# Hybrid decoder trunk, two layers on one core: weight remainders and weight-block sums on VectorE, own semaphores for late cells, the sigmoid first in the gated output, layer 1's right sums in its projection

## The reference

```python
for i in range(2):
    h = rmsnorm(x, norm_mix[i])
    x = x + (even_mixer if i % 2 == 0 else odd_mixer)(h, ...)
    h = rmsnorm(x, norm_ffn[i])
    g = causal_dwconv(h @ w_gate[i], conv_w[i], conv_b[i])        # width 3, d_ff = 2816
    x = x + (gelu(g) * (h @ w_up[i])) @ w_down[i]
    gate = sigmoid(rmsnorm(x, norm_ple[i]) @ w_ple_gate[i])
    x = x + gate * (p[i] @ w_ple_proj[i])
```

## Time and profile before

| | before |
|---|---|
| median of 3 executions | 3092.41 us (3090.21 to 3092.66) |
| the profiled execution | 3093.49 us, its span 3091.7 us |
| mean granted TensorE clock | 0.993 |
| PE busy | 97% |
| DVE, ACT, POOL busy | 72%, 47%, 41% |
| DMA, mean | 113 GB/s |

### The profile page before, as it was taken

One profiled execution on the slowest core, in us unless ns is written; L12 is line 12 of the kernel. 1 busy time (PEld: TensorE's weight loads), 2 busy tenths in 40 slices (PEclk: granted clock), 3 DMA queues, 4 the chain that ended last, 5 costly groups with the idle time before them and its releaser, 6 DMA issues. The chain is left out here.

```text
span 3091.7 us, 44204 instructions
## 1 busy us (share of the span) xinstructions
PE 2989.6 (97%) x14830; PEld 2497.6 (81%) x14830; DVE 2238.8 (72%) x3533; ACT 1441.8 (47%) x3127; POOL 1269.5 (41%) x837
## 2 busy tenths in 40 slices
PE   7999999999999999999999999999999999999999
PEld 6778888978878878878888888899887887878877
DVE  5599997889377888789843331899548877879852
ACT  4385436878253333344432211888534333334431
POOL 3105545465235555511122545677325555630020
PEclk9999999999999999999999999999999999999999
DMA  5323334222314563375211334333122465266411
GB/s 176 127 58 101 99 123 108 50 56 68 130 66 145 156 139 108 133 262 194 84 55 41 105 97 140 82 68 75 48 90 91 157 157 138 82 227 225 154 55 48
DMA packets 288087, 349.07 MB, mean 113 GB/s; under 512 B 88316, under 2 KB 181292, under 8 KB 287916
## 3 DMA queue, kind: packets, MB, share of 16 engines
q1 hardware_dynamic: 274860, 312.27, 32.1%
q0 software_dynamic: 13056, 34.60, 5.2%
HBM read 268.70 MB, written 112.20 MB: 123 GB/s over the span
## 5 line engine op out<-in xcount | busy, mean ns | idle before, releaser
L2171 DVE TENSOR_SCALAR_CACHE_REDUCE k_x<-k_x,l0in_cand,l0in_want 128x384 bf16<-128x384 f32 (+1 forms) x186 | 174.9, 1003 | 1.2 <-DVE l0in_before L2166 0.2
L78 PE MATMUL l1in_acc<-k_w_lo,k_hi 128*128 128x512 f32 x384 | 150.9, 393 | 2.4 <-PEq L99 2.4
L80 PE MATMUL l1in_acc<-k_w_hi,k_hi 128*128 128x512 f32 x384 | 150.1, 391 | 0.0
L79 PE MATMUL l1in_acc<-k_w_hi,k_lo 128*128 128x512 f32 x384 | 150.0, 391 | 0.0
L2662 POOL TENSOR_TENSOR l0ff_w_lo<-l0ff_raw_g,l0ff_w_hi 128x512 fp32r<-128x512 f32 x64 | 90.7, 1424 | 133.2 <-ACT l0ff_w_hi L2520 132.6
L2662 POOL TENSOR_TENSOR l1ff_w_lo<-l1ff_raw_g,l1ff_w_hi 128x512 fp32r<-128x512 f32 x64 | 90.8, 1426 | 132.8 <-ACT l1ff_w_hi L2520 132.1
L2549 ACT ACTIVATE k_x<-k_x 128x512 f32<-128x512 f32 x88 | 55.6, 632 | 187.9 <-DVE k_x L2754 175.7
L721 DVE TENSOR_TENSOR l1in_sq<-l1in_out 128x512 f32<-128x512 f32 x32 | 38.4, 1201 | 107.9 <-ACT l1in_out L658 107.9
L1632 DVE TENSOR_TENSOR l1dil_pt_lo<-l1dil_ring,l1dil_pt_hi 128x512 fp32r<-128x512 f32 x192 | 102.0, 553 | 4.7 <-ACT l1dil_pt_hi L1568 2.3
L1648 DVE CUSTOM_DVE_ANT_0 l1dil_s<-l1dil_s,l1mix_sliding 128x128 f32<-128x128 f32 (+7 forms) x128 | 97.3, 761 | 8.5 <-PE l1dil_s L1732 5.6
L2710 DVE TENSOR_TENSOR l0ff_w_lo<-l0ff_raw_u,l0ff_w_hi 128x512 fp32r<-128x512 f32 x65 | 62.3, 958 | 56.6 <-ACT l0ff_w_hi L2520 56.6
(11 more groups left out here) (739 smaller groups left out, 11093.4 us busy)
## 6 DMA issues: line engine op xcount, KB each, us to landing
...
k_raw<-in_w_in_odd SPq DMA_DIRECT2D x24, 512.0 KB, 4.0
l0ff_raw_g<-in_w_gate SPq DMA_DIRECT2D x11, 1024.0 KB, 5.5
l0ff_raw_u<-in_w_up SPq DMA_DIRECT2D x11, 1024.0 KB, 6.5
...
l1ff_raw_g<-in_w_gate SPq DMA_DIRECT2D x11, 1024.0 KB, 5.5
```

Source lines behind the costliest of these rows:

```text
L78: pe.matmul(out, a_hi, b_lo, start=start, stop=False)
L79: pe.matmul(out, a_lo, b_hi, start=False, stop=False)
L80: return pe.matmul(out, a_hi, b_hi, start=False, stop=stop)
L2171: tick(dve.tensor_scalar(hits[:, cols], score[:, cols], cand[:, i:i + 1].bitcast(F32), want[:, i:i + 1], ALU.is_ge, ALU.add, accum_out=exc ...
```

## The change

1. In `ffn_stage` all lows go to VectorE, but for step 4 of group 0 and those of the down projection; so do all weight sums of groups 1 to 10. POOL keeps the sums of group 0.
2. The right sums stay in the feed-forward stage in layer 0 alone (`here`). Layer 1's are issued in its projection stage, copies behind the lows of strips 1 and 2, adds behind those of strips 3 and 4, chunks 0 to 2 of each.
3. The cells that are loaded late get semaphores of their own (`a11_late`, `a12_late`), which are waited for at cells 6, 7 and 8.
4. In the gated output ACT does unit 0's sigmoid before the squares, two squares go between the first two splits, the other two to unit 1, the later splits one unit later; TensorE runs the gate matmuls of unit 1 before unit 0's projection; VectorE's product waits for the projection itself.

```diff
@@ projection_stage, POOL
                     low(CH * s + c)
+                    if s in (1, 2) and c < 3:
+                        right_sums.copy(pool, 3 * s - 3 + c)
+                    if s in (3, 4) and c < 3:
+                        right_sums.add(pool, 3 * s - 9 + c)
@@ ple_stage, ACT
             p_round(1)
-            for t in range(ROOTS, NT):
-                feed.square(act, t)
+            act.wait_ge(begun, 1)
+            act.activation(sg[:, 0, :], ps_g[:, 0, :], ACT.Sigmoid).then_inc(sig_done, 1)
             split(0)
+            for t in range(ROOTS, ROOTS + 2):
+                feed.square(act, t, junk[:])
             split(1)
             for i, (s, t) in enumerate(UNITS):
                 if i in TURN_AFTER:
                     feed.round(act, TURN_AFTER[i])
...
-                if i < CH - 2:
-                    split(2 + i)
+                if i == 1:
+                    for t2 in range(ROOTS + 2, NT):
+                        feed.square(act, t2, junk[:])
+                if 0 < i <= CH - 2:
+                    split(1 + i)
@@ ple_stage, VectorE
                 dve.wait_ge(sig_done, i + 1)
+                dve.wait_ge(filled, i + 1)
@@ ple_stage, TensorE
             p_turn(0)
             p_turn(1)
+            gate(1)
             for i, (s, t) in enumerate(UNITS):
                 if i >= 2:
                     pe.wait_ge(prod_done, i - 1)
...
+                    gate(i)
@@ ffn_stage, SP
-                    load_part(a11, (0, 0), range(7, 8), a11_in)
-                    load_part(a12, (0, 1), range(6, 8), a12_in[0])
+                    load_part(a12, (0, 1), range(6, 8), a12_late)
+                    load_part(a11, (0, 0), range(7, 8), a11_late)
@@ ffn_stage, POOL
-                if q + L < Q and (q + L) % 2 == 0:
-                    low(q + L)
-                if n in (11, 12) and grp + 1 < NG:
-                    add_weights(grp + 1, 7, n - 11)
-                if n in (11, 13) and grp + 1 < NG:
-                    add_weights(grp + 1, 5, (n - 11) // 2)
-                if grp and n in (0, 1):
-                    add_weights(grp, 6, n)
-                if n in (3, 4):
+                if grp == 0 and n in (3, 4):
                     add_weights(grp, 3, n - 3)
-                if n in (2, 12) and 1 <= grp <= 6:
+                if here and n in (2, 12) and 1 <= grp <= 6:
                     i = 2 * ((grp - 1) % 3) + (n == 12)
                     right_sums.copy(pool, i) if grp <= 3 else right_sums.add(pool, i)
@@ ffn_stage, VectorE
                 if r == 0 and k == 0:
-                    dve.wait_ge(a11_in, 16 * 8)
+                    dve.wait_ge(a11_in, 16 * 7)
...
-                if q + L < Q and (q + L) % 2 == 1:
+                if q + L < Q:
                     low(q + L)
+                if n in (11, 12) and grp + 1 < NG:
+                    add_weights(grp + 1, 7, n - 11)
+                if n in (11, 13) and grp + 1 < NG:
+                    add_weights(grp + 1, 5, (n - 11) // 2)
+                if 0 < grp < NG and n in (0, 1):
+                    add_weights(grp, 6, n)
+                if 0 < grp < NG and n in (3, 4):
+                    add_weights(grp, 3, n - 3)
```

More of the change, by code:

```diff
@@ L152, in square @@
             act.wait_ge(self.squared, n)
-        act.activation(self.norm.junk, self.src[:, t, :], ACT.Square, accum_out=self.norm.ss[:, t:t + 1]).then_inc(self.squared, 1)
+        act.activation(junk if junk is not None else self.norm.junk, self.src[:, t, :], ACT.Square, accum_out=self.norm.ss[:, t:t + 1]).then_inc(self.squared, 1)
     def prepare(self, pool):
@@ L1205, in p_turn, with gate @@
                 mm.then_inc(p_turned, 1)
+            def gate(i):
+                s, t = UNITS[i]
+                tok = buf.slot(t)
+                for k in range(KD):
+                    if s == 1 and t == 0 and k % 2 == 0:
+                        pe.wait_ge(lo_ready, k // 2 + 1)
+                    mm3(pe, ps_g[:, i % 2, :], hi[:, tok, k, :], lo[:, tok, k, :], buf.x_hi[s][:, k, :], buf.x_lo[s][:, k, :], k == 0, k == KD - 1)
             p_turn(0)
             p_turn(1)
+            gate(1)
             for i, (s, t) in enumerate(UNITS):
@@ L1211, in _ @@
                     pe.wait_ge(prod_done, i - 1)
-                if t >= AHEAD:
-                    feed.ready(pe, t)
-                tok = buf.slot(t)
-                for k in range(KD if i else 0):
-                    if s == 1 and t == 0 and k % 2 == 0:
-                        pe.wait_ge(lo_ready, k // 2 + 1)
-                    mm3(pe, ps_g[:, i % 2, :], hi[:, tok, k, :], lo[:, tok, k, :], buf.x_hi[s][:, k, :], buf.x_lo[s][:, k, :], k == 0, k == KD - 1)
+                    if t >= AHEAD:
+                        feed.ready(pe, t)
+                    gate(i)
                 if s == 1 and t == 0:
@@ L2442, in _ @@
                     sp.wait_ge(filled, Q - 2)
-                    load_part(a11, (0, 0), range(8, 11), a11_in)
+                    load_part(a11, (0, 0), range(8, 11), a11_late)
                     load_part(a12, (0, 1), range(8, 9), a12_in[1])
@@ L2709, in low, with add_weights @@
                 dve.wait_ge(w_hi_done, q - buf.BEGUN + 1)
-                dve.tensor_tensor(buf.ring_lo[q % R][:], operand(q), buf.ring_hi[q % R][:].bitcast(F32), ALU.subtract).then_inc(w_lo_done[1], 1)
+                if q == 6:
+                    dve.wait_ge(w_lo_done[0], 3)
+                dve.tensor_tensor(buf.ring_lo[q % R][:], operand(q), buf.ring_hi[q % R][:].bitcast(F32), ALU.subtract).then_inc(w_lo_done[q % 2], 1)
+            def add_weights(grp, f, m):
+                n = 8 * grp + SUM_AT[f, m]
+                if f == 7:
+                    dve.wait_ge(raw_in[m], 16 * grp)
+                    dve.wait_ge(w_lo_done[m], 7 * grp + 1)
+                    dve.tensor_tensor(buf.piece(m, 0, 0), buf.piece(m, 0, 0), buf.piece(m, 1, 0), ALU.subtract).then_inc(w_sum, 1)
+                elif f == 5:
+                    dve.wait_ge(w_sum, n - 1)
+                    dve.tensor_tensor(buf.piece(m, 1, 0), buf.piece(m, 1, 0), buf.piece(m, 1, 1), ALU.add).then_inc(w_sum, 1)
+                elif f == 6:
+                    dve.wait_ge(w_sum, 8 * grp + SUM_AT[7, m])
+                    if grp == 0:
+                        dve.wait_ge(kept_stored[0], 16 * 6)
+                    dve.tensor_tensor(tmp[m], buf.piece(m, 1, 1), buf.piece(m, 0, 0), ALU.subtract).then_inc(w_sum, 1)
+                else:
+                    dve.wait_ge(w_sum, 8 * grp + SUM_AT[6, m])
+                    dve.wait_ge(w_lo_done[m], 7 * grp + 2)
+                    dve.tensor_tensor(buf.piece(m, 0, 1), buf.piece(m, 0, 1), tmp[m], ALU.subtract).then_inc(w_sum, 1)
             def corner(grp, m):
@@ L2779, in sum_left @@
                 if r == 0 and k == 0:
-                    dve.wait_ge(a11_in, 16 * 8)
+                    dve.wait_ge(a11_in, 16 * 7)
                 if r == 0 and k in (0, 8, 9):
                     n = max(k - 7, 0)
-                    dve.wait_ge(a12_in[n], 16 * (8, 1, 2)[n])
+                    dve.wait_ge(a12_in[n], 16 * (6, 1, 2)[n])
+                if r == 0 and k == 6:
+                    dve.wait_ge(a12_late, 16 * 2)
+                if r == 0 and k == 7:
+                    dve.wait_ge(a11_late, 16)
                 if r == 0 and k == 8:
-                    dve.wait_ge(a11_in, 16 * KB2)
+                    dve.wait_ge(a11_late, 16 * 4)
                 if r == 2 and k == 0:
@@ L3065, in trunk @@
                     Stage.used.extend(kept_stored + [filled])
-                    ffn_stage(nc, L + "ff", x, buf, ple, right_sums[layer], a["conv_w"][layer], a["conv_b"][layer], ident, acts, kept_stored, filled, begun)
+                    ffn_stage(nc, L + "ff", x, buf, ple, right_sums[layer], a["conv_w"][layer], a["conv_b"][layer], ident, acts, kept_stored, filled, begun, even)
                 recycle(nc)
```

18 lines of the change are left out of this document (11 added, 7 removed).

## The result

| | before | changed |
|---|---|---|
| median | 3091.49 us (4 runs, 3090.21 to 3092.66) | 3116.68 us (4 runs, 3114.69 to 3118.21) |
| ratio | | 1.0081, 95% interval 1.0069 to 1.0093 |
| profiled execution | 3093.49 us, span 3091.7 | 3118.21 us, span 3115.7 |
| mean granted clock | 0.993 | 0.987 |

The account below looks back on a forecast made before the run. TensorE was taken as the bound, busy 2989.6 of 3091.7 us. Terms -6.3 - 5.2 + 18.8 + 4 - 4.5 - 5.8 + 8 + 6 = +15.0 on the profiled 3093.5, stated as 3107 us, range 3075 to 3130.

Parts of the forecast that it names:

- the weight work on VectorE: Feed-forward: moving lows and weight sums from POOL removes the middle stretches' pauses, -6.3 us in layer 0, -5.2 in layer 1.
- the burst in layer 0: Feed-forward: unpaced, six right-sum copies then six adds go out together and delay raw-block loads, +18.8 us and +4 for clock.
- the gated output: Both layers: POOL's lows wait for all roots, so p loads late and gate(3) waits; +6 +2 and +4 +2 us.
- VectorE fits: Feed-forward: VectorE's 48 rows per group take 33.1 of 38.0 us, so it does not become the bound.
- the undisturbed row: 0.69 us per VectorE row without POOL's reads; the rival keeping the means had 47.5 us a group, 3280, milder 3127, chance 0.12.
- +18.8 + 4: Layer 0 feed-forward: late raw blocks of groups 1 and 2 cost 18.8 us, two falls of the clock 4.
- Group 1's first block lands near 932: Layer 0 feed-forward: that raw block lands near 932 instead of 925 beside the copies, holding VectorE's low and an eviction, +4.9 us.
- the 6.7: Layer 0 feed-forward: group 2's second block follows on the same queue another 11 us later, costing +6.7 us.
- In-order blocking: Feed-forward: VectorE waits in order at a group's first low for the raw block, with evictions of TensorE's banks queued behind.
- on POOL, where nothing else was urgent: Feed-forward: where each group's first low stood before the change, so its wait for the raw block held up nothing urgent.
- Layer 1's right sums: Layer 1 projection: issued behind the lows while POOL stands idle 88 us, they cost 0, between -1 and +2 us.
- The late cells: Start of the down projection: own semaphores end sum_left(0)'s wait for two unread cells, -4.5 us in layer 0, -5.8 in layer 1.

Follow-up runs that it names:

- the paced runs: Runs holding right-sum DMAs until TensorE has filled their steps; the first, the changed kernel with layer 0's twelve paced, measured 3092.93 us, ratio to before 1.0008.

## Why the prediction was right, and where its sizes were off

**The direction and the mechanisms.** Forecast 3107 in a range of 3075 to 3130, measured 3116.7. All three mechanisms that the sum rested on are in the trace and hold when each is undone or made alone: the weight work on VectorE is a gain (-16.1 alone), the burst in layer 0 a loss larger than it (23.8 come back when it is paced, and it costs 15.4 with its copies alone), the gated output a loss in both layers (+16.6 alone).

**VectorE fits.** 48 rows of 0.69 us were to give 33.1 of 38.0 us, 87%; the window 1011 to 1320 has 83%. The choice between the mean of before and the undisturbed row was the right one: with POOL idle the lows have a mean of 0.69. By the rule of the Trainium skill cited in the forecast ("SBUF — State Buffer", Who interferes with whom) this was to be expected, and the trace agrees: 0.69 with POOL idle, and in before 1.11 beside POOL against 0.68.

**The burst was mis-sized**, +18.8 + 4 against 15.8 + 9.2 = 25.0 of pauses and some 4 of half clock, and that the sum came so near is in part luck: the first pause was put at 4.9 and was 15.8, what follows the second burst was put at 5.9 + 6.7 + 1.3 = 13.9 and was 9.2.

The step that failed is "Group 1's first block lands near 932". It was split at 938.7. Three things are in the difference between the pauses. First, the forecast didn't use its own price: 13.4 us from the issue at 920.1 is 933.5 already, and 5.5 us to landing against 3 of records leave 2.5 more for the start. Second, the copy's record was read from one microsecond, 0.164 us. Over the whole burst, from 901 to 939 us, the queue has

```profile
q0 software_dynamic: 2208, 8.65, 73.8%
```

that is 38 x 16 x 0.738 / 2208 = 0.203 us a record, and 28 us of all engines where the sum had 21.6. Third, TensorE, 2.8 us earlier than in before, came to the bank at 925.7, not at 928.5, and went on 2.8 us after the split where the sum had 1.4 (932 + 1.4 - 928.5 = 4.9). (The forecast's formula for a raw block's record, 16 x 0.915 / 946, lacks the 3 us of its window; its result of 0.046 is right.) The block's records start late too: q1 has 19 records from 921 to 923 us and 126 from 923 to 926. An estimate with these figures and the raw record's 0.051 of 930 to 931 us, 923.5 + 64 x (0.203 + 0.051), gives 940 for a DMA engine that has copies to the end.

Behind the second pause the up block's split came 9.2 us after the gate block's (996.62 and 987.45), but its low was done just before its step, so the 6.7 didn't come.

**In-order blocking** was given as the reason why the burst would hurt. It is what ends the wait in the changed kernel, but a small part of its length: the run with the burst on the kernel before has a pause of 16.3 us with the low on POOL, and the estimate there leaves some 3.5 us to VectorE's order. That the low stood "on POOL, where nothing else was urgent" is true and of little use: TensorE needs that low itself one step later. In before the block was split at 925.35, POOL had its low at 927.3, and the step that uses it began at 931.3: the look-ahead stood 4 us of lateness, and the block came 13 to 20 late. What the order costs without a burst is in the paced runs, pauses of 1.5 to 2.2 us at the same bank in layer 0.

**The gated output** came as worked out: lows at S + 15.9 (15.3 forecast), load of p at S + 25.9 (25.3), unit 3 at S + 32.2 (30.6), +9.1 and +6.4 (8 and 6). Not seen was the second chain behind it, the third chunk's split ahead of unit 1's sigmoid on ACT. It changed nothing in the sum, since the first chain was longer, but it halved what undoing the first gave.

**Layer 1's right sums, 0 with an upper bound of 2**: the projection stage is longer by 1.1 to 5.6 us than in before in the seven traces that have them there. The six other traces that don't have them there are within 0.2 us of before. The step that failed looked at POOL's idle time only; what ends late there is the weight load beside the copies.

**The late cells, -4.5 - 5.8.** Alone they gave -7.7, and nothing in company. The sum had counted a consequence (VectorE late, so the stores and the cells late) as a cause of its own, beside the term that removes it. Part of layer 1's missing gain is also a new pause of 1.9 us at its group 1, where VectorE's order holds a bank as in layer 0 (the 2.2 of its group 0 stands where before had three pauses by lows and t_lo, 1.1, 1.4 and 0.8).

**Open.** Why VectorE lags by about 5 us to the end of layer 1's stage in before, and no longer when the adds are gone from its middle, wasn't tried. Nor was what is left in layer 1's gated output, or a place for layer 0's right sums outside of the feed-forward stage.
